# Hybrid Hyena and attention encoder layer on one core: the filter network and the first filters moved ahead of the memory keys and the input transposes

## The reference, cut to what matters

```python
h = rms_norm(x, norm_mix)
u_hy, q, k, v = split(h @ w_in)
# filter network, independent of x and of the memory
a = sin(freq0 * (z @ w1 + b1));  a = sin(freq1 * (a @ w2 + b2))
filt = (a @ w3).reshape(L, 2, 2, 512) * exp(-t * deltas)      # order, forward/backward, channel
k2 = concat([fwd, 0, bwd[:0:-1]]);  k2 = k2 / (sum(abs(k2), axis=0) + eps)
k_f = rfft(k2)                                                # one spectrum per order
y_hy = hyena_mixer(u_hy, ..., k_f)                            # fft_long_conv twice, with gates
x = x + concat([norm(y_hy), norm(gqa_mixer(q, k, v))]) @ w_out
m = rms_norm(mem, norm_mem)                                   # keys m @ w_k, values m @ w_v
x = x + memory_cross_attn(rms_norm(x), m, ...)
x = x + hier_moe(rms_norm(x), ...)
```

## Time and profile before

| | |
|---|---|
| runs | 940.27, 945.86, 947.08 us |
| median | 945.86 us |
| profiled execution, span from first to last instruction | 944.0 us |
| TensorE, VectorE, ScalarE, GpSimd busy | 88%, 66%, 48%, 16% of the span |
| mean granted clock of TensorE | 0.857 of full speed |
| transfers | 159.80 MB, 169 GB/s on average |

### The profile page before, as it was taken

The page is one execution under the profiler, slowest core; times in us unless marked ns, Lnnn a source line. Parts: engine busy times, 40 slices in busy tenths (PEclk is TensorE's granted clock), DMA queues, the critical chain, the costliest instruction groups (busy, mean ns, idle before and its releaser), DMA issues.

```text
span 944.0 us, 10345 instructions
## 1 busy us (share of the span) xinstructions
PE 830.4 (88%) x3436; PEld 632.4 (67%) x3436; DVE 622.0 (66%) x874; ACT 448.7 (48%) x653; POOL 155.2 (16%) x148
## 2 busy tenths in 40 slices
PE   5889989968788999999989799269999999999970
PEld 3555656755685666668877568257888888888860
DVE  5585836894797125543333724758999999999944
ACT  6641313211416343332225714147878878878840
POOL 0057141513400000000000000020121231231210
PEclk8999989979989555555999798569999999999985
DMA  8530202200212000000222005969999999999917
GB/s 285 198 90 23 67 22 67 68 22 1 89 45 90 1 0 1 0 1 1 90 89 70 21 22 205 344 209 338 381 399 397 398 402 398 398 399 400 383 70 289
DMA packets 64440, 159.80 MB, mean 169 GB/s; under 512 B 2871, under 2 KB 4791, under 8 KB 63960
## 3 DMA queue, kind: packets, MB, share of 16 engines
q1 hardware_dynamic: 58936, 139.46, 40.9%
q0 software_dynamic: 5472, 19.93, 5.4%
HBM read 146.79 MB, written 12.58 MB: 169 GB/s over the span
## 4 chain that ended last, share of the span: by engine, by line
PE 71%; DVE 16%; ACT 5%; DMA 4%; issue 2%; POOL 1%; SPq 1%; ACTq 0%; DVEq 0%; POOLq 0%
PE bank L1667 16%; PE bank L1612 12%; PE bank L1910 10%; PE bank L1912 9%; PE bank L1911 9%; PE bank L1798 6%; PE bank L1619 4%; PE bank L1905 2%; DVE w_lo L973 1%; DMA x_in<-in_x 1%; DMA y_back<-y_dram 1%; PE bank L1680 1%; PE bank L1850 1%; ACT junk L611 1%; DVE sd L1134 1%
## 5 line engine op out<-in xcount | busy, mean ns | idle before, releaser
L1546 DVE TENSOR_TENSOR e_lo<-slot,e_hi 128x1024 fp32r<-128x1024 f32 x192 | 221.4, 1219 | 9.9 <-ACT e_hi L876 9.6
L876 ACT ACTIVATE e_hi<-slot 128x1024 fp32r<-128x1024 f32 x192 | 188.2, 1062 | 5.4 <-PE bank L1912 5.4
L973 DVE TENSOR_TENSOR w_lo<-w_raw,w_hi 128x1024 fp32r<-128x1024 f32 x42 | 51.1, 1233 | 85.7 <-ACT w_hi L638 85.6
L1910 PE MATMUL bank<-e_hi,hgT_hi 128*128 128x512 f32 x256 | 102.2, 399 | 3.8 <-DVE hgT_lo L1558 3.8
L1912 PE MATMUL bank<-e_hi,hgT_lo 128*128 128x512 f32 x256 | 100.8, 394 | 0.0
L1911 PE MATMUL bank<-e_lo,hgT_hi 128*128 128x512 f32 x256 | 100.7, 393 | 0.0
L638 ACT ACTIVATE w_hi<-w_raw 128x1024 fp32r<-128x1024 f32 x42 | 44.0, 1062 | 108.1 <-DMA w_raw<-in_w_in 54.4
L1271 DVE TENSOR_REDUCE small<-bank 128x1 f32<-128x512 f32 x32 | 22.1, 691 | 75.8 <-PE bank L1798 75.8
L793 ACT ACTIVATE pT<-bank 128x512 f32<-128x512 f32 x32 | 19.1, 598 | 87.4 <-PE bank L1619 87.3
L1612 PEld LDWEIGHTS bank<-qkv,pT 128*128 128x128 f32 x256 | 58.4, 333 | 0.2 <-issue 0.2
L1619 PEld LDWEIGHTS bank<-ident,pr 128*128 128x128 f32 x160 | 26.5, 203 | 47.8 <-issue 38.6
(11 more groups left out here) (312 smaller groups left out, 1710.3 us busy)
## 6 DMA issues: line engine op xcount, KB each, us to landing
slot<-in_w_gate SPq DMA_DIRECT2D x16, 2048.0 KB
slot<-in_w_up SPq DMA_DIRECT2D x16, 2048.0 KB, 15.6
slot<-in_w_down SPq DMA_DIRECT2D x16, 2048.0 KB
w_raw<-in_w_in SPq DMA_DIRECT2D x18, 512.0 KB, 3.6
w_raw<-in_w_out SPq DMA_DIRECT2D x8, 512.0 KB, 3.8
y_back<-y_dram SPq DMA_DIRECT2D x8, 512.0 KB, 7.7
w_raw<-in_w_k_mem SPq DMA_DIRECT2D x4, 512.0 KB, 6.4
x_in<-in_x SPq DMA_DIRECT2D x4, 512.0 KB, 9.4
```

What stands on the lines that cost most here:

```text
L876: act.activation(e_hi[buffer(b, j)][:], slot[slot_][:, 1024 * part:1024 * (part + 1)], ACT.Copy).then_inc(s_ehi, 1)
L973: dve.tensor_tensor(w_lo[slot_][:], w_raw[slot_][:], w_hi[slot_][:].bitcast(F32), ALU.subtract)\
L1546: dve.tensor_tensor(e_lo[slot_][:, at_], slot[slot_][:, at_], e_hi[buffer(b, j)][:].bitcast(F32), ALU.subtract)\
L1910: pe.matmul(dst, act_hi, w_hi_, start=first, stop=False)
```

## The change

The same instructions are issued, save two table loads on ScalarE; what changes is their order, one wait and three addresses.

- SP: the loads of `w3` and `decay` go ahead of the first weight pieces and x. The load of `idft` (the inverse transform's table, 1 MB) moves from the first stage to just ahead of piece 13, behind waits for the last filter sums of order 1.
- TensorE: the filter products of order 0 come right behind the second network product.
- ScalarE: first sine ahead of the memory's high parts, second sine ahead of the weights' high parts; the absolute values of order 0 stand around the squares of x.
- VectorE: second range reduction ahead of `memT_lo`; all filter evictions and sums of order 0 ahead of the low part of piece 3.
- Buffers: `fabs1` and `fb1` lie where `idft` lies later; the squares' unused output has an area of its own.

```diff
-    jobs += [("mk", j) for j in range(MT)] + [("hT", 0, k) for k in range(KT)] + filt(0, range(4))
+    jobs += filt(0, range(4)) + [("mk", j) for j in range(MT)] + [("hT", 0, k) for k in range(KT)]
...
-        fabs = [at("fabs0", 172, [P, 2, CH]), at("fabs1", 140, [P, 2, CH])]
+        fabs = [at("fabs0", 172, [P, 2, CH]), at("fabs1", 116, [P, 2, CH])]
...
-        fb = [at("fb0", 192, [P, 2, CH]), at("fb1", 136, [P, 2, CH])]
+        fb = [at("fb0", 192, [P, 2, CH]), at("fb1", 112, [P, 2, CH])]
...
             sp_.dma_start(mem_raw[:], a["mem"][0].rearrange("(j p) d -> p j d", p=P)).then_inc(ld["mem"], 16)
+            sp_.dma_start(w3[:], a["filt_w3"][0]).then_inc(ld["w3"], 16)
+            sp_.dma_start(decay[:], a["decay"]).then_inc(ld["decay"], 16)
             for n in range(NSLOT):
                 load_piece(n)
             for i in range(TT):
                 sp_.dma_start(x_in[:, i, :], x_src[:, i, :]).then_inc(ld["x"], 16)
-            sp_.dma_start(w3[:], a["filt_w3"][0]).then_inc(ld["w3"], 16)
-            sp_.dma_start(decay[:], a["decay"]).then_inc(ld["decay"], 16)
...
-            sp_.dma_start(idft[:], a["idft"]).then_inc(ld["idft"], 16)
             for n in range(NSLOT + 1, len(pieces)):
+                if n == first_piece["g1"] + 1:
+                    sp_.wait_ge(s_spdm, 8)
+                    sp_.wait_ge(s_l1, 8)
+                    sp_.dma_start(idft[:], a["idft"]).then_inc(ld["idft"], 16)
                 load_piece(n)
...
+            first_junk = at("first_junk", 24, [P, D])[:]
...
+            sine(0, a1)
             for j in range(KT // 2):
                 job = ("memT", j)
...
-            sine(0, a1)
+            sine(1, a2)
             weight_hi(0, 3)
+            abs_pair(0, 0)
+            abs_pair(0, 1)
             act.wait_ge(ld["x"], 16 * TT)
             rms(x_in, 4, TT, TT)
+            abs_pair(0, 2)
+            abs_pair(0, 3)
             act.wait_ge(ld["mem"], 16)
             rms(mem_raw, 0, MT, TT + MT)
-            sine(1, a2)
             weight_hi(3, 1)
...
-            weight_hi(4, 3)
-            abs_pair(0, 0)
-            abs_pair(0, 1)
-            weight_hi(7, 1)
-            abs_pair(0, 2)
-            abs_pair(0, 3)
+            weight_hi(4, 4)
...
             mlp(1)
-            chunk_jobs("mk", memT_hi, memT_lo, split=lambda k: ("memT", k // 2))
-            hT_jobs(0, x_in, lambda k: pe.wait_ge(s_xn, TT))
             pe.wait_ge(s_sin, 2)
             pe.wait_ge(ld["w3"], 16)
             filter_jobs(0, range(4))
+            chunk_jobs("mk", memT_hi, memT_lo, split=lambda k: ("memT", k // 2))
+            hT_jobs(0, x_in, lambda k: pe.wait_ge(s_xn, TT))
             chunk_jobs("mv", memT_hi, memT_lo)
```

More of the change, by code:

```diff
@@ L610, in rms @@
                 for i in range(n):
-                    act.activation(fb_flat, src[:, i, :], ACT.Square, accum_out=small[:, first + i:first + i + 1])\
+                    act.activation(first_junk, src[:, i, :], ACT.Square, accum_out=small[:, first + i:first + i + 1])\
                         .then_inc(s_sq, 1)
@@ L984, in _ @@
             free(dve.tensor_copy(small[0:1, 399:400], cols[0:1, 0:1]), ("mlp", 0))
+            range_reduce(1)
+            dve.wait_ge(s_arg, 2)
+            free(dve.tensor_copy(small[0:1, 399:400], cols[0:1, 0:1]), ("mlp", 1))
             for j in range(KT // 2):
@@ L992, in _ @@
                 free(ins, job)
[L993 to L1008, removed]
             def filters(o, t):
@@ L1015, in filters @@
                     dve.wait_ge(s_abs, 4 * o + t - 1)
-                if o == 0 and t == 1:
-                    dve.wait_ge(s_hi, KT // 2)
                 wait_filled(dve, fwd)
@@ L1068, in outer_taps @@
                                                   ALU.mult, ALU.add), job)
+            dve.wait_ge(ld["decay"], 16)
             filters(0, 0)
             filters(0, 1)
[L1072 to L1077, removed]
+            weight_lo(0, 3)
+            l1_add(0, 0)
+            filters(0, 2)
+            l1_add(0, 1)
+            filters(0, 3)
+            dve.wait_ge(s_rms, 1)
+            link(dve.reciprocal(small[:, 20:24], small[:, 20:24]))
+            for i in range(TT):
+                dve.tensor_scalar(x_in[:, i, :], x_in[:, i, :], small[:, 20 + i:21 + i], None, ALU.mult).then_inc(s_xn, 1)
+            l1_add(0, 2)
+            l1_add(0, 3)
+            dve.wait_ge(s_rms, 2)
+            dve.reciprocal(small[:, 16:18], small[:, 16:18]).then_inc(s_xn, 1)
+            weight_lo(3, 1)
+            for k in range(KT):
+                split_lo(("hT", 0, k), hT_lo[:, k, :], hT_hi[:, k, :], col("norm_mix", k))
+            weight_lo(4, 4)
             l1_norm(0)
```

## The result

The changed kernel took **957.5 us**, median of four runs (956.72 to 961.36); the kernel before, timed beside it, 945.33. Ratio 1.0134, 95% interval 1.0106 to 1.0161: slower by about 12 us. The forecast was 952.2 with a range to 958. The profiled execution has a span of 955.4 us, 11.4 more than before.

The account below looks back on a forecast made before the run. Time was taken to be set where TensorE waits or runs at its lower clock. Span 944.0 + 5.8 (L1 product) + 1.7 (inverse table) - 1.2 (root table) = 950.3, plus 1.9 allowance: 952.2 us; range 944.5 to 958.

Parts of the forecast that it names:

- the largest term of the sum: First stage up to the L1 product: product comes +5.8 us later, +2 with low ends, +10 with high ends.
- step 2: VectorE's queue ahead of piece 3: its low part ends at 41.5 us, transposes of x start 11.4 us later.
- Step 1: Sines and first filters, earlier: second sine ends at 18.1 us instead of 28.7, eighth filter product at about 27.7.
- Step 3: Transposes of x to L1 product: TensorE waits over 3 us for piece 4; L1 product at 68.7 us against 63.06.
- Step 4: Inverse table's load ahead of piece 13: that chain 3.5 us late, part given back at the restart, net +1.7 us.
- Step 5: ScalarE's table loads: the 1.28 us load at 244.22 goes, -1.2 us (0 to -1.3).
- (a): Rival at 18, 41, 55 and 128 us: TensorE keeps the full clock, not slower, 945.5 us; 17%.
- (b): Rival: two waits add up in full, with slowed sums, low-clock transposes, no table-load time back; 957.0 us; 20%.
- (c): Rival from 46 to 63 us: VectorE's filter chain was the bound, L1 product near 59, kernel 940.7 us; 5%.
- (d): Rival: the change of order does nothing, all covered elsewhere save the table load; 944.7 us; 5%.

Follow-up runs that it names:

- the second clock experiment: Changed kernel with 36 useless transposes on TensorE between the second network product and the filter products; ratio 1.0143 to the kernel before.
- the extra sine: Changed kernel with one single-element sine added on ScalarE, so the root table must be loaded again before the head norms; ratio 1.0097 to the kernel before.

## Why the prediction was right, and where it was not

The direction, the place and the mechanism were right, and the range held the time, by half a microsecond. That it did is in part luck: the largest term of the sum came out above even its own high end of +10. The chance of slower by over 1%, which is what came, had only 28%. **The failed step is step 2, a term that was mis-sized: +5.8 us at the L1 product where +10.9 was measured.** (Its own last line, 68.7 against 63.06, is +5.6.)

**Step 1.** Second sine forecast to end at 18.1, measured 18.2. Filter products: three slow and five fast were forecast, 9.6 us; all were slow, 14.0. The transposes of the second clock experiment show that this changed little.

**Step 2.** By its own entries, forecast and measured end (taken where the next one starts): fourth eviction 24.9, 26.1; three low parts 28.4, 31.7; second eviction pair 30.4, 33.6; two sums 33.8, 36.0; pair 35.1, 37.3; scaling 38.0, 42.2; four sums 40.8, 45.1; low part of piece 3 42.1 (41.5 taken), 46.4. Of the 4.9 us that are missing 1.2 come from the products, 2.1 from the low parts and 2.0 from the scaling beside GpSimd; 1.0 came back, as one of the two sums was spared; and 0.6 is the step from 42.1 down to the 41.5 that was taken for a third product at the full clock, which did not come. I had found GpSimd's price for the sums (1.76 against 0.69) and did not charge it to the two longer operations that stand in the same stretch. The sentence with the bound, "with four more sums slowed 44", looked for it at the wrong operations, and four sums at 1.0 us more each would have made it 46, not 44. The Trainium skill, "SBUF — State Buffer" (section "SBUF: two separate sides"), has VectorE and GpSimd share one port pair that whichever comes first holds for a whole instruction, and counts to it VectorE operations with two SBUF inputs and its faster two-port modes; by that the subtractions and the scaling would both have been charged. The trace agrees: 3.47 against 5.64 and 2.74 against 4.90 us, while evictions from PSUM stay at 0.67 to 0.69.

**Step 3.** TensorE waits 3.64 us for piece 3, not over 5, since the slow filter products kept it longer at work. Piece 3's matmuls 4.5 us (5.1 forecast, at the low level as said); transposes to first value product 8.8 (9.0), with a wait of 3.80 ("over 3"); from there to the L1 product 14.2 (13.1). Right but for 1.1 us, of which 0.8 are piece 4's matmuls (4.9 us at the low level, from 59.72 to 64.60, for 4.1).

**Step 4.** Low part of piece 13 later by 3.5 us against the L1 products, as forecast (107.96 before, 122.27 after, 10.8 of it the shift); wait before the spectra 3.96, before gate 1 2.32. Net at the forward product +1.8 (92.2 against 90.4), forecast +1.7. Right, with part of the restart's cost given back as assumed; but with the extra sine, where the order is the same up to there, the distance is 90.7, so that the close match is partly luck.

**Step 5.** -1.2 forecast, about -0.4 measured: the term forgot that a chain that comes earlier can meet GpSimd. The root follows its table load at once in every trace; the drain of the page cited there did not appear.

From the L1 product to the end of the span the length was to be within 3 us of its old one: 881.4 against 880.9.

**The rivals.** (a) needed the full clock; given to the filter products, it brought nothing, so its first item (1.7 us) was wrong, while piece 3 at the full clock (2.4 us in it) did pay, 1.6 us, when its wait was short. (b) gave nearly the measured time, 957.0, by things that did not happen: the four sums took 0.7 us each, the transposes ran at full speed, and the table load's cost was partly given back. (c) and (d) fall: VectorE's queue for piece 3 was the bound, not the filter chain. The time given for (c), 940.7, lies within 1% of the old one, so its 5% did not belong to "faster by over 1%".

## What to carry to other kernels

Before moving work earlier, write down the whole in-order queue of each engine between the old and the new place, and charge each VectorE operation that reads only SBUF for GpSimd's work beside it, not only the kind that a trace happens to show slowed. A gap filled on TensorE is worth nothing if another engine's queue sets where the gap ends; one line that takes the awaited operation out from behind four that can wait gave back 5 us at the L1 product (and about half of the loss in time, 1.0052 against 1.011), where doubling the speed of 14 us of products gave none.

## What the hardware showed that was not expected

- After standing for 4.35 us, TensorE worked for over 18 us without a pause (18.27 to 36.7) at the lower level; its filter products, 64 rows deep, did not bring the clock back, and it came back during 128-row fp32r matmuls. After 18 transposes and a gap of 2.24 us nearly all of them were slow as well; after 36 and a gap of 0.27 us none was. The Trainium skill, "TensorE: Matmul & The Clock Gate" (section "What's actually happening"), has activity of the engine release its clock; for this stretch the trace does not agree.
- GpSimd's sums and differences take 1.25 us alone (23.00 to 25.48, while VectorE evicts from PSUM) and 2.1 to 2.3 us beside VectorE's subtractions: both lose.
- The memory rows landed 5.1 us after their issue before the change, 5.9 in the changed kernel and 7.1 in its repetition, so the same code varied by more than the two kernels differ. That the loads of `w3` and `decay`, now issued right behind them, slow them is not shown.
